# Last norm of a mixture-of-experts encoder: output tiles of sequence 1 stored by indirect scatters, order on VectorE and ScalarE rearranged

## What is computed

```python
x = layer_norm(DEEPNORM_ALPHA * x + jnp.dot(mixed, w_out), ln1_g, ln1_b)
x = layer_norm(DEEPNORM_ALPHA * x + grouped_moe(x, w_router, router_bias, w_gate, w_up, w_down), ln2_g, ln2_b)

def layer_norm(x, g, b):
    xf = x.astype(jnp.float32)
    mu = jnp.mean(xf, -1, keepdims=True)
    xc = xf - mu
    var = jnp.mean(xc * xc, -1, keepdims=True)
    return (xc * lax.rsqrt(var + LN_EPS) * g + b).astype(x.dtype)
```

## Time and profile before

| | us |
|---|---|
| median of 3 runs | 1008.17 |
| the three runs | 1004.71, 1008.17, 1012.00 |
| span of the profiled execution | 1005.1 |
| PE busy in it | 919.4 (91%) |
| VectorE busy | 616.7 (61%) |
| ScalarE busy | 534.2 (53%) |
| GpSimd busy | 177.8 (18%) |

### The profile page before, as it was taken

How to read it: one execution, slowest core, us unless ns; L and a number is a source line. 1 busy time by engine, 2 the same in 40 slices (tenths; PEclk the granted TensorE clock), 3 DMA queues, 4 the chain that set the end, 5 groups by cost and what they waited for, 6 DMA issues and landing times.

```text
span 1005.1 us, 15974 instructions
## 1 busy us (share of the span) xinstructions
PE 919.4 (91%) x4959; PEld 744.9 (74%) x4960; DVE 616.7 (61%) x1182; ACT 534.2 (53%) x1008; POOL 177.8 (18%) x260
## 2 busy tenths in 40 slices
PE   5899999899989999989973999999999999999982
PEld 5777888687877788867742788888888888888850
DVE  5443644655744573465698989989456494564684
ACT  4343565542445565554343878877446584464460
POOL 4300002001000011100011234435222232221301
PEclk9998999989999999989975999999999999999996
DMA  8740114116342352310755999999868697674524
GB/s 252 120 108 22 42 43 130 61 43 201 115 104 84 112 183 54 116 42 22 281 215 171 352 362 394 389 374 392 275 203 260 197 342 228 218 248 116 150 107 193
DMA packets 95119, 183.95 MB, mean 183 GB/s; under 512 B 24064, under 2 KB 52975, under 8 KB 95072
## 3 DMA queue, kind: packets, MB, share of 16 engines
q1 hardware_dynamic: 80496, 137.91, 38.3%
q0 software_dynamic: 14144, 43.88, 16.4%
q10 hardware_dynamic: 432, 1.57, 0.4%
HBM read 159.85 MB, written 28.70 MB: 188 GB/s over the span
## 4 chain that ended last, share of the span: by engine, by line
PE 41%; DVE 15%; issue 6%; DMA 4%; ACT 3%; DVEq 1%; SPq 0%; ACTq 0%; POOL 0%; POOLq 0%
PE O L2009 9%; PE C L1728 7%; PE C L1730 7%; PE C L1729 7%; DVE split_main L1594 6%; PE O L1909 3%; PE T L1962 2%; PE S L1763 2%; PE T L1884 2%; PE S L1969 1%; PE T L1792 1%; DMA mixing<-in_w_out 1%; DMA mixing<-acc_dram 1%; ACT split_main L1092 1%; DVE mixing L1675 1%
## 5 line engine op out<-in xcount | busy, mean ns | idle before, releaser
L1594 DVE TENSOR_TENSOR split_main<-mixing,split_main 128x1024 fp32r<-128x1024 f32 x188 | 217.7, 1221 | 35.0 <-ACT split_main L1092 32.3
L1092 ACT CAST split_main<-mixing 128x1024 fp32r<-128x1024 f32 x188 | 186.4, 1050 | 17.2 <-PE C L1730 7.1
L1728 PE MATMUL C<-split_main,split_aux 128*128 128x512 f32 x368 | 143.9, 391 | 1.3 <-DVE split_aux L1600 1.3
L1730 PE MATMUL C<-split_main,split_aux 128*128 128x512 f32 x368 | 143.9, 391 | 0.0
L1729 PE MATMUL C<-split_main,split_aux 128*128 128x512 f32 x368 | 143.6, 390 | 0.0
L1728 PE MATMUL C<-split_main 128*128 128x512 f32 (+1 forms) x320 | 130.4, 407 | 3.5 <-DVE split_main L1434 3.0
L2009 PE MATMUL O<-split_main,split_aux 128*128 128x512 f32 x552 | 132.7, 396 | 0.0
L1729 PE MATMUL C<-split_main 128*128 128x512 f32 (+1 forms) x320 | 121.6, 380 | 0.0
L1730 PE MATMUL C<-split_main 128*128 128x512 f32 (+1 forms) x320 | 121.4, 379 | 0.0
L2009 PEld LDWEIGHTS O<-split_main,split_aux 128*128 128x128 f32 x552 | 100.2, 188 | 23.4 <-DVE split_aux L1615 4.7
L1728 PEld LDWEIGHTS C<-split_main,split_aux 128*128 128x128 f32 x368 | 69.5, 189 | 15.9 <-issue 1.5
(11 more groups left out here) (341 smaller groups left out, 1435.3 us busy)
## 6 DMA issues: line engine op xcount, KB each, us to landing
mixing<-in_w_down SPq DMA_DIRECT2D x64, 512.0 KB, 8.2
mixing<-in_w_gate SPq DMA_DIRECT2D x64, 512.0 KB, 9.1
mixing<-in_w_up SPq DMA_DIRECT2D x64, 512.0 KB, 6.1
mixing<-in_w_in SPq DMA_DIRECT2D x20, 512.0 KB, 3.8
mixing<-in_w_out SPq DMA_DIRECT2D x16, 512.0 KB, 4.1
mixing<-in_w_mem_kv SPq DMA_DIRECT2D x8, 512.0 KB, 6.1
mixing<-in_w_in SPq DMA_DIRECT2D x16, 256.0 KB, 3.7
x_dram<-x_nat POOLq DMA_DIRECT2D x8, 512.0 KB, 2.9
```

What stands on the lines that cost most here:

```text
L1092: nc.scalar.copy(wu[0][:, w, :], raw[:, w, :]).then_inc(unit_hi, 1)
L1594: nc.vector.tensor_tensor(wu[1][:, w, :], raw[:, w, :], wu[0][:, w, :].bitcast(F32), ALU.subtract).then_inc(unit_lo, 1)
L1728: ins = nc.tensor.matmul(out_ap, st[0], mvg[0], start=first, stop=False)
L1730: ins = nc.tensor.matmul(out_ap, st[1], mvg[0], start=False, stop=last)
```

## The change

The tiles 4 to 7, all of sequence 1, are no longer stored by SP. GpSimd stores them by indirect scatters (`keep_rows`), each with a column of row numbers `kept`, in which the rows that the last two expert tiles touch are made too large, so that the bounds check drops them. VectorE makes `kept` with four more small instructions. The fix rows of sequence 1 then write other rows than these and wait for no landing. On VectorE products 0 to 2 move in between the statistics; `total`'s hidden part moves ahead of the first chain of roots; the rest of tile 3 moves ahead of the second chain, the rest of `fix[0]` right behind it, and `fix[1]`'s ahead of tile 7's. On ScalarE the copies for `total`'s transposes and `fin_ones` move ahead of the wait for the roots.

```diff
+        kept = rows8[:, 960:960 + NT].bitcast(I32)
...
@@ SP
-            for t in range(FIN_PE, TT):
+            for t in range(FIN_PE, NT):
                 sp.wait_ge(fin_y, t - FIN_PE + 1)
-                sp.dma_start(out[t // NT][0, (t % NT) * P:(t % NT + 1) * P, :], fin[t]).then_inc(out_stored[t // NT], 16)
+                sp.dma_start(out[0][0, t * P:(t + 1) * P, :], fin[t]).then_inc(out_stored[0], 16)
@@ GpSimd
+            def keep_rows(t):
+                pool.wait_ge(fin_y, t - FIN_PE + 1)
+                nc.gpsimd.indirect_dma_start(out[1][0], bass.IndirectOffsetOnAxis(kept[:, t - NT:t - NT + 1], 0), fin[t], None,
+                                             bounds_check=S - 1, oob_is_err=False).then_inc(out_stored[1], 16)
+
+            pool.wait_ge(kept_ready, 1)
+            pool.wait_ge(fix_ready, 1)
+            fix_rows(1, 0)
+            for t in range(NT, TT - 1):
+                keep_rows(t)
+            pool.wait_ge(fix_ready, 2)
+            fix_rows(1, 1)
+            keep_rows(TT - 1)
             pool.wait_ge(out_stored[0], 16 * NT)
             for i in range(FIX):
-                pool.wait_ge(fix_ready, i + 1)
                 fix_rows(0, i)
-            pool.wait_ge(out_stored[1], 16 * NT)
-            for i in range(FIX):
-                fix_rows(1, i)
@@ ScalarE
             fin_tile(6)
+            tile_hidden(total, last=True)
+            nc.scalar.copy(fin_ones, ones_b[0:1, :]).then_inc(fin_diags, 1)
             act.wait_ge(fin_rooted, 1)
-            nc.scalar.copy(fin_ones, ones_b[0:1, :]).then_inc(fin_diags, 1)
             for t in range(FIN_PE):
                 nc.scalar.activation(fin_diag[t], ident[:, :], ACT.Copy, scale=rstd[:, t:t + 1]).then_inc(fin_diags, 1)
-            tile_hidden(total, last=True)
             fin_tile(7)
@@ VectorE
-            for t in range(FIN_DVE):
+            last_rows, in_last = nv[:, 8:9], rows8[:, 976:992]
+            link(nc.vector.tensor_scalar(last_rows, rows8[:, 528 + NE - 1:528 + NE], float(P), float(-FIX * P), ALU.mult, ALU.add))
+            link(nc.vector.tensor_scalar(in_last, rows8[:, 576:592], last_rows, None, ALU.is_ge))
+            link(nc.vector.tensor_tensor(in_last[:, 0:NT], in_last[:, NT:TT], in_last[:, TT + NT:2 * TT], ALU.max))
+            nc.vector.scalar_tensor_tensor(kept, in_last[:, 0:NT], 4.0 * S, tokf[:, 0:NT], ALU.mult, ALU.add).then_inc(kept_ready, 1)
+            for t in range(FIN_DVE - 1):
                 fin_stats(t)
+                fin_product(t)
+            fin_stats(FIN_DVE - 1)
             fix_sum(0, before, wcur)
+            tile_first(total, last=True)
             link(nc.vector.tensor_scalar(nv[:, 0:4], mvv[:, 0:4, 1], EPS / ALPHA ** 2, None, ALU.add))
             rsqrt(rstd[:, 0:4], 4)
             nc.vector.memset(seed[:, 11:12], 0.0).then_inc(fin_rooted, 1)
-            fin_product(0)
-            tile_first(total, last=True)
-            for t in range(1, 5):
+            for t in range(FIN_DVE - 1, 5):
                 fin_product(t)
             fix_sum(1, total, wlast)
             for t in range(5, TT + 1):
                 fin_product(t)
+            dve.wait_ge(fin_gain, gained[0])
+            fin_rest(3, fin_y)
             dve.wait_ge(fin_squared, n_act)
             link(nc.vector.tensor_scalar(nv[:, 0:n_act], fin_ssq, 1.0 / D, EPS / ALPHA ** 2, ALU.mult, ALU.add))
             rsqrt(fin_root, n_act)
+            fin_rest(TT, fix_ready)
             fin_product(TT + 1)
+            for t in range(FIN_DVE, TT - 1):
+                fin_rest(t, fin_y)
             dve.wait_ge(fin_gain, gained[0])
-            fin_rest(3, fin_y)
-            fin_rest(TT, fix_ready)
-            for t in range(FIN_DVE, TT):
-                fin_rest(t, fin_y)
             fin_rest(TT + 1, fix_ready)
+            fin_rest(TT - 1, fin_y)
```

More of the change, by code:

```diff
@@ L515, in build_kernel @@
         fix_stored = sem("fix_stored")
+        kept_ready = sem("kept_ready")
         out_stored = [sem(f"out_stored{s}") for s in range(NSEQ)]
```

## The result

The first comparison gave a median of 1006.67 us (22 runs, 1001.14 to 1011.67) for the changed kernel against 1011.50 us (22 runs, 1002.45 to 1019.49) for the kernel before. The ratio is 0.9959, 95% interval 0.9940 to 0.9978: faster by 0.4%, some 4.1 us. Two later comparisons gave 0.9966 (0.9946 to 0.9986) and 0.9978 (0.9948 to 1.0008). The forecast was 1004.3 us, 3.9 us less than before. The ratios and their intervals leave out runs more than 1.5% above the fastest of the same kernel; the medians of all 22 runs stand 4.8 us apart.

What follows compares the result with a forecast made beforehand. The bound was taken as VectorE's end plus the tail to the last scatter, then a fixed 8.9 us. VectorE's end -2.9 and tail -1.0 give -3.9: 1004.3 us from 1008.17, range 1000.0 to 1009.3.

Steps and rivals of the forecast that it cites:

- VectorE ahead of `total`: VectorE before the last expert tile: load gaps take products and four small instructions, so L1611 starts 2.9 us earlier.
- VectorE's and ScalarE's order behind it: After the last expert tile: VectorE ends at 988.6, not 991.53; ScalarE's squares are ready at 976.8, 0.9 us to spare.
- Rival (d): ScalarE becomes the bound at copies or squares; 2 us late there loses 1.1, gain 2.8, 1005.4 us; chance 0.07.
- What the gap costs: PE idles 3.08 us before its transposes until VectorE's L1611 releases it; L1611 would start 2.9 us earlier.
- GpSimd's pace: Scatters beside VectorE's rests: over 0.83 us after a rest's end, next starts 0.31 later, keeping VectorE's 1.2 us.
- rival (a): A scatter just misses the gap and waits a further VectorE instruction, pitch 2.4 us; gain 2.6, 1005.6 us; chance 0.13.
- the tail: From VectorE's end to the last scatter's start: 3.7 us where it was 4.67, a gain of 1.0.
- My margin of 0.06 us: GpSimd beside VectorE: the next scatter starts 1.14 us after a rest's end, VectorE's next end comes at 1.20.
- Tile 2's landing: ScalarE's last store to `out[0]`, issued about 2.9 us before the earlier 986.2, lands at 986.0, long before the final scatters.
- Behind the last scatter: From the last scatter's start through landing and GpSimd's drain to the span's end: a fixed 8.9 us, unchanged.
- Rival (c): GpSimd's 5.3 us drain grows with scatters under way; four more could double it: +1.4 us, 1009.6; chance 0.08.
- Rival (b): Five scatters each stop VectorE for 0.96 us; it ends 4.8 us later, +0.9 in all, 1009.1 us; chance 0.05.

Runs made afterwards that it cites:

- after_again: Changed kernel, no edit, run and profiled a second time; one of the two later comparisons (0.9966 and 0.9978 against the kernel before).
- after_both: Changed kernel plus two bf16 bias matmuls for fp32 (tiles 0 to 2, parts made by GpSimd) and `fix[1]`'s rest waiting for tile 6; 0.9971 against the kernel before.
- before_third: Kernel before, no edit, against itself, for a third profile; ratio 1.0011 (0.9973 to 1.0048).
- before_fourth: Kernel before, no edit, one execution for a fourth profile; 1014.17 us.
- order_only: Changed kernel with SP's plain stores and GpSimd's waits for landings taken back, VectorE's and ScalarE's new order kept; 0.9998 against the kernel before.
- after: Changed kernel, its first profile, span 1008.5 us; the first comparison gave 0.9959 against the kernel before.
- before_cheap: Kernel before with the fp32 bias matmul of tiles 0 to 2 replaced by two bf16 ones, parts made by GpSimd; 1.0015 against the kernel before.
- after_link: Changed kernel with one more wait on VectorE, `fix[1]`'s rest waiting for tile 6's semaphore; 0.9976 against the kernel before.
- before_again: Kernel before, no edit, one execution for a second profile; 1018.25 us.

## Why the prediction was right, and where it was not

**VectorE ahead of `total`: right.** `total`'s product starts 18.2 us behind T0 in all four profiles of the changed kernel, 21.1 to 21.3 in the four of before: 2.9 to 3.1 us against 2.9. The load gaps took the products and the four small instructions. The cover is thin, as said: VectorE waited 0.97 us for PE in front of `total`'s product in after_again, and not at all in the first profile of the changed kernel. In after_both, where GpSimd's new work held VectorE, 1.78 us of the gap came back.

**VectorE's and ScalarE's order behind it: right.** VectorE's end moved from 46.9 to 44.0 at full clock. ScalarE waited 2.82 us for the roots and had the last squares ready 32.1 us behind T0, where I had 976.8 - 944.62 = 32.2. Rival (d) did not occur.

**What the gap costs: sized too small.** I priced it by one profile as its own length. In two of the four profiles of before the clock was at the lower level for 3 to 7 us from about the end of the gap (before_third from 966.6, before_fourth from 966.2), and VectorE's end was at 48.2 and 49.5. So the mean gain at VectorE's end is 47.9 - 44.0 = 3.9 us. In those two profiles, though, VectorE's end is not what the last scatter waited for.

**GpSimd's pace: wrong.** The step "the next one starts at e + 1.14, and the next end of VectorE is e + 1.20. So they keep VectorE's pace" failed. The next VectorE instruction starts 0.08 us before the end of the one in flight, at e + 1.12, and a scatter that starts behind that waits for the end of this one. That is rival (a), which I gave 0.13, once in each profile. Where tile 2's store holds nothing up, the tail is 993.13 - 988.12 = 5.0 us (after_again), not 3.7, and no shorter than the 4.67 of before. The last scatter's 49.0 us behind T0 are those of rival (a), 993.6 - 944.62. With a gap made by the extra wait the tail is 3.75. My margin of 0.06 us also rested on a slip: VectorE's rest ended at 991.53 - 1.20 = 990.33 and not at 990.43, so the scatter of before was over 0.93 us behind it. By that row the next one would start at e + 1.24, behind e + 1.20, and the row already spoke for rival (a). In the first profile of the changed kernel the scatters beside VectorE end 0.84 to 0.92 us behind such an end.

**Tile 2's landing: wrong.** "They wait for `out[0]`: ... at 986.0, long before" took the clock and the landing time of one profile for granted. Where the clock stayed up it was right: order_only has the store at 38.6 us behind T0, as forecast (986.2 - 2.9 - 944.62 = 38.7). Tile 2's store came 41.6 to 49.5 us behind T0 in before and gated all four scatters in three of four profiles; in the changed kernel it came at 42.4 to 46.6 and gated the last two in three of four. What bounds before in three of its four profiles is thus PE's part of the last norm by way of this store and its landing, and not VectorE. What the change gains there is, by these rows, 1.5 us of an earlier store in the mean (46.3 to 44.8, with single ones 41.6 to 49.5, so this term is not sure) and 2.5 us of two scatters taken from behind it.

**Behind the last scatter: nearly right.** I had the same 8.9 us; it is 8.7 in after and after_again. Landing takes 0.6 to 0.9 us less: the last scatter is now one of sequence 0, and 3.3 us is also what order_only and before_cheap show, which end on sequence 1 as before does. The drain ends 0.4 to 0.8 us later behind the landing. In after_again:

```profile
L268 POOLq DRAIN  x1: 11043/11043/11043, 990.5 to 990.5; - x1
L268 SPq COMPARE_BRANCH  x1: 38/38/38, 995.8 to 995.8; - x1
```

990.5 + 11.04 - 995.8 = 5.7 us, against 5.3 in before. Rival (c) has the sign right and about a tenth of the size.

**Rival (b) fell.** Five rests, with three scatters and the start of a fourth beside them, took 6.06 to 6.07 us, 1.28 + 4 x 1.20: scatters did not hold VectorE. The rule of the Trainium skill (SBUF — State Buffer, the single rule) that the second to start blocks for the whole instruction agrees with the trace on GpSimd's side, with 2.07 against 0.96 us. On VectorE's side a scatter does not do it: in after_link one of 0.96 us began ahead of a rest, and the five rests together took only 0.19 us more, 0.12 of which is the added wait's own cost (in before an instruction that waited so stood 1.32 us behind its forerunner, at 981.75 and 983.07, in place of 1.20). GpSimd's own arithmetic does: in after_both it held VectorE's small instructions for 2.7 us, as shown above, which is what the rule says.

So one part of the sum held and one did not. Where tile 2's store holds up none of the last scatters, the change gains 60.5 - 57.7 = 2.8 us, where I had 3.9; the step that failed is the tail, 5.0 us and not 3.7. The measured ratios give 4.1, 3.4 and 2.2 us, with intervals that hold both 2.8 and 3.9. By the profiles the rest up to their 3.8 comes from executions in which the clock falls early, where the gap and tile 2's store cost before more than the changed kernel; that is the account which fits, but no measured time shows it, since the kernels with the cheaper bias did not come out as it expected. That the forecast's 3.9 met the measured size is in part luck.

## What to carry to other kernels

Before a forecast rests on one profile, ask what in it depends on a clock that may stand at another level in the next execution, and price the chain that would then end last. Where a queue holds both work that waits for a late landing and work that does not, put the waiting work last: it costs nothing when the landing is early and saves each other item's time when it is late. A scatter issued beside back-to-back VectorE instructions is paced by their starts, so count its start against the next instruction's start, not against the end of the one in flight. And before small work is moved to an idle engine, look at what the engine beside it does at that moment: here GpSimd's two instructions cost VectorE 2.7 us in one execution.

## What the runs showed of the hardware that was not expected

The granted clock of PE fell from 1.00 to 0.50 while PE was busy without a break in fp32 matmuls, 4 to 9 us behind the first of them in seven of the eight profiles of the two kernels, and only at the last pair, 12 us behind the first, in the remaining one. After 3.20 us without work PE came back at the lower clock in before_fourth, and at the full one after 3.08 us in the first profile of before and after 3.29 us in before_again. A GpSimd scatter of 128 row numbers is issued in 0.96 us whether it stores all rows or only some, and at 1.27 us from start to start. Such scatters left VectorE's pitch at 1.20 us, while a GpSimd cast of 1x1024 and a subtraction of 1x1024 held VectorE's small instructions until 0.03 us behind their own ends (after_both).
